# Attention with a sink: the sink as one more score column that TensorE writes, and queries scaled by ScalarE

## The reference, cut to what matters

```
sk = jnp.broadcast_to(sink...reshape(kv, g, 1, 1), s.shape[:-1] + (1,))
p = jax.nn.softmax(jnp.concatenate([s, sk], axis=-1), axis=-1)
return p[..., :-1]
```

## Time and profile before

| what | value |
|---|---|
| device time, median of 3 runs (lowest to highest) | 782.83 us (782.64 to 782.89) |
| device time of the profiled execution | 782.79 us |
| span, first to last instruction, in the profile | 780.9 us |
| mean granted TensorE clock | 0.996 |
| busy, PE / PEld / DVE / ACT / POOL | 738.8 / 573.5 / 583.1 / 502.8 / 50.4 us |

### The profile page before, as it was taken

The page is one execution under the profiler, slowest core; times in us unless marked ns, Lnnn a source line. Parts: engine busy times, 40 slices in busy tenths (PEclk is TensorE's granted clock), DMA queues, the critical chain, the costliest instruction groups (busy, mean ns, idle before and its releaser), DMA issues.

```text
span 780.9 us, 10972 instructions
## 1 busy us (share of the span) xinstructions
PE 738.8 (95%) x4019; PEld 573.5 (73%) x4020; DVE 583.1 (75%) x968; ACT 502.8 (64%) x834; POOL 50.4 (6%) x36
## 2 busy tenths in 40 slices
PE   4999999899999999999999999989999999999994
PEld 2557877457966888888769788845698788888874
DVE  4258386986666899999858746879666789999965
ACT  3048693574457777777646678457456887777852
POOL 0001352000000000000000135200000000000000
PEclk9999999999999999999999999999999999999998
DMA  9963034977338899999864113096831189999902
GB/s 365 423 244 109 14 121 168 423 271 272 109 116 366 316 369 366 379 368 350 327 240 153 58 52 103 33 382 211 303 128 55 55 327 379 375 363 376 370 18 84
DMA packets 33489, 186.26 MB, mean 239 GB/s; under 512 B 5136, under 2 KB 6288, under 8 KB 16400
## 3 DMA queue, kind: packets, MB, share of 16 engines
q1 hardware_dynamic: 33424, 185.42, 62.9%
HBM read 182.79 MB, written 2.62 MB: 237 GB/s over the span
## 4 chain that ended last, share of the span: by engine, by line
PE 74%; DVE 11%; ACT 9%; issue 4%; DMA 1%; ACTq 0%; DVEq 0%; SPq 0%
PE psum L875 22%; PE psum L1022 11%; PE psum L904 11%; PE psum L1224 5%; PE psum L989 4%; PE psum L705 3%; PE psum L927 3%; PE psum L853 2%; DVE att L2260 1%; ACT split L1415 1%; PE psum L741 1%; PE psum L1092 1%; PE psum L756 1%; PE psum L888 1%; PE psum L1106 1%
## 5 line engine op out<-in xcount | busy, mean ns | idle before, releaser
L2049 DVE TENSOR_TENSOR split<-ring,split 128x2048 fp32r<-128x2048 f32 x96 | 219.9, 2291 | 26.8 <-ACT split L1540 25.3
L1540 ACT CAST split<-ring 128x2048 fp32r<-128x2048 f32 x96 | 183.6, 1913 | 21.9 <-PE psum L904 14.5
L875 PE MATMUL psum<-split,y_hi 128*128 128x512 f32 x512 | 160.8, 395 | 0.4 <-ACT selT L1513 0.4
L875 PEld LDWEIGHTS psum<-split,y_hi 128*128 128x128 f32 x512 | 93.7, 188 | 18.6 <-issue 0.5
L875 PE MATMUL psum<-split,y_lo 128*128 128x512 f32 x256 | 100.1, 391 | 0.0
L1022 PE MATMUL psum<-ring_r,hT_hi 128*128 128x512 f32 x216 | 73.2, 393 | 0.0
L904 PE MATMUL psum<-split,hidT 128*128 128x512 f32 x256 | 69.7, 394 | 1.8 <-DVE hidT_lo L2054 1.8
L904 PEld LDWEIGHTS psum<-split,hidT 128*128 128x128 f32 x256 | 47.3, 188 | 14.2 <-DVE hidT_lo L2054 4.8
L875 PEld LDWEIGHTS psum<-split,y_lo 128*128 128x128 f32 x256 | 48.1, 188 | 10.2
L2490 POOL TENSOR_TENSOR ud<-const,da_hi 128x1024 fp32r<-128x1024 f32 x12 | 27.3, 2293 | 397.8 <-DVE da_lo L2150 390.3
L1022 PEld LDWEIGHTS psum<-ring_r,hT_hi 128*128 128x128 f32 x216 | 40.0, 188 | 9.0 <-issue 0.7
(11 more groups left out here) (314 smaller groups left out, 1425.6 us busy)
## 6 DMA issues: line engine op xcount, KB each, us to landing
ring<-in_w_gu SPq DMA_DIRECT2D x64, 1024.0 KB, 5.8
ring<-in_w_ada SPq DMA_DIRECT2D x40, 1024.0 KB, 6.6
ring<-in_w_down SPq DMA_DIRECT2D x32, 1024.0 KB, 5.7
ring<-in_w_rows SPq DMA_DIRECT2D x12, 1024.0 KB, 5.1
ring<-in_first SPq DMA_DIRECT2D x8, 1024.0 KB, 14.7
ring<-in_w_out SPq DMA_DIRECT2D x8, 1024.0 KB, 5.8
ring<-in_w_xbc SPq DMA_DIRECT2D x8, 800.0 KB, 9.1
par<-in_par SPq DMA_DIRECT2D x1, 1728.0 KB, 14.1
```

The source lines that it names most:

```text
L875: last = pe.matmul(dst, x[:, g, t, :], w[:, j, :], start=(t == 0 and i == 0), stop=(t == KD - 1 and i == 2))
L1540: act.copy(splits[unit_split(n)][:, 0, :], slot(key)).then_inc(raised("whi", l, p), 1)
L2049: tt(lo, slot(unit_key(l, p, n)), hi.bitcast(F32), ALU.subtract).then_inc(raised("wlo", l, p), 1)
```

## The change: the sink as a score column

A K = 1 matmul (ones by the sink) writes the sink into column w of the unit's bank, w being the number of keys, after the other matmuls of the pair have been issued. Maximum and exponential run over w + 1 columns where t = 0, so that the row sum holds the sink. The queries are scaled by 0.125 when ACT copies them, so that scores come out of TensorE with the factor in and the maximum is directly the bias of the exponential. The steps that handled the sink on DVE and ACT, the factor step, and the signal `es` are gone. Units with a sink need 385 columns for probabilities, so `probs` is a function: a tile that starts 16 words ahead of `hT`, in which slots 0 to 3 have 385 words each and slots 4 to 7 lie where they did.

```diff
+        with ExitStack() as shared:
+            prob_space = sb("prob_space", [P, 16 + KD * TOK], c=shared)
+        sb("prob_front", [P, 16])
...
-        nsink = sb("nsink", [P, DEPTH, NH])
...
-            att = sb("att", [P, 6, len(HEADS)], c=mix)
+            att = sb("att", [P, 3, len(HEADS)], c=mix)
...
-            probs = hT
+            def probs(u, a, b):
+                at = 12 + u % 8 * TOK + min(u % 8, 4)
+                return prob_space[:, at + a:at + b]
...
+            def sink(l, v, kv):
+                m, _, _, i = HEADS[2 * v]
+                w = P if m == 0 else TOK
+                at = T_SINK + 2 * kv + i
+                return pe.matmul(bank(("scores", l, 2 * v + kv))[:, w:w + 1], ones[0:1, :], tab[0:1, l, at:at + 1], start=False,
+                                 stop=True, skip_group_check=True)
...
@@ tensor, scores
-                            if m == 0:
+                            if m == 0 and t == 1:
                                 last.then_inc(*filled(("scores", l, 2 * v + kv)))
+                        if m == 0 and t == 0:
+                            for kv in range(NKV):
+                                sink(l, v, kv).then_inc(*filled(("scores", l, 2 * v + kv)))
...
                                 for kv in range(NKV):
-                                    last = pe.matmul(dsts[kv][:, other], ident_b, mask_b[:, m - 1, other], start=False,
-                                                     stop=True, skip_group_check=True)
-                                    last.then_inc(*filled(("scores", l, 2 * v + kv)))
+                                    pe.matmul(dsts[kv][:, other], ident_b, mask_b[:, m - 1, other], start=False,
+                                              stop=True, skip_group_check=True)
+                                for kv in range(NKV):
+                                    sink(l, v, kv).then_inc(*filled(("scores", l, 2 * v + kv)))
...
@@ scalar, turn_qk
-                            act.copy(qkT[:, 3 * t:3 * t + 3, m * P:(m + 1) * P], src).then_inc(*was_read(key))
+                            act.activation(qkT[:, 3 * t:3 * t + 2, m * P:(m + 1) * P], src[:, 0:2, :], ACT.Copy, scale=SCALE)
+                            act.copy(qkT[:, 3 * t + 2, m * P:(m + 1) * P], src[:, 2, :]).then_inc(*was_read(key))
@@ scalar, scores
-                        w = P if m == 0 else TOK
+                        w = (P if m == 0 else TOK) + (t == 0)
...
-                            act.activation(probs[:, u % 8, 0:w], src[:, 0:w], ACT.Exp, bias=att[:, 1, u:u + 1],
-                                           scale=SCALE, accum_out=att[:, 2, u:u + 1]).then_inc(*was_read(key))
-                        if t == 0:
-                            act.activation(att[:, 3, 2 * v:2 * v + 2], att[:, 3, 2 * v:2 * v + 2], ACT.Exp)\
-                                .then_inc(sig["es"], 1)
+                            act.activation(probs(u, 0, w), src[:, 0:w], ACT.Exp, bias=att[:, 0, u:u + 1],
+                                           accum_out=att[:, 1, u:u + 1]).then_inc(*was_read(key))
@@ vector, scores
-                            ins = dve.tensor_reduce(att[:, 0, u:u + 1], src[:, 0:P if m == 0 else TOK], AX.X, ALU.max,
-                                                    negate=True)
-                        ins.then_inc(dve_step, 1)
-                        dve.wait_ge(dve_step, dve_steps())
-                        if t == 0:
-                            sink = nsink[:, l, :].rearrange("p (v i) -> p i v", i=2)[:, i, :]
-                            stt(att[:, 1, two], att[:, 0, two], SCALE, sink, ALU.mult, ALU.min).then_inc(dve_step, 1)
-                            dve.wait_ge(dve_step, dve_steps())
-                            tt(att[:, 3, two], att[:, 1, two], sink, ALU.subtract).then_inc(sig["nb"], 1)
-                        else:
-                            ts(att[:, 1, two], att[:, 0, two], SCALE, None, ALU.mult).then_inc(sig["nb"], 1)
+                            ins = dve.tensor_reduce(att[:, 0, u:u + 1], src[:, 0:w], AX.X, ALU.max, negate=True)
+                        ins.then_inc(sig["nb"], 1)
@@ vector, scale
-                        den = att[:, 2, two]
-                        if t == 0:
-                            dve.wait_ge(sig["es"], per["es"] * l + sum(1 for x in range(v + 1) if HEADS[2 * x][1] == 0))
-                            tt(att[:, 4, two], den, att[:, 3, two], ALU.add).then_inc(dve_step, 1)
-                            dve.wait_ge(dve_step, dve_steps())
-                            den = att[:, 4, two]
-                        dve.reciprocal(att[:, 5, two], den).then_inc(dve_step, 1)
+                        dve.reciprocal(att[:, 2, two], att[:, 1, two]).then_inc(dve_step, 1)
...
-                            ins = ts(probs[:, u % 8, 0:w], probs[:, u % 8, 0:w], att[:, 5, u:u + 1], None, ALU.mult)
+                            ins = ts(probs(u, 0, w), probs(u, 0, w), att[:, 2, u:u + 1], None, ALU.mult)
```

More of the change, by code:

```diff
@@ L539, in build @@
                 ("dt_r", 1), ("da", 1), ("bss", 3), ("brs", 3), ("prep", 3), ("ud", 3), ("ud_lo", 3), ("da_lo", 1), ("xd", 3), ("yx", 3),
-                ("mhi", 4), ("mlo", 4), ("mixhi", 4), ("ohi", 1), ("olo", 1), ("wb", 3), ("dtd", 1), ("skip", 3), ("seg", 6), ("in_hi", PARTS + 2), ("in_lo", PARTS + 3), ("zs", 1), ("nb", PAIRS), ("es", PAIRS // 2), ("pn", PAIRS), ("yz", 1), ("yrs", 1), ("yn", 1),
+                ("mhi", 4), ("mlo", 4), ("mixhi", 4), ("ohi", 1), ("olo", 1), ("wb", 3), ("dtd", 1), ("skip", 3), ("seg", 6), ("in_hi", PARTS + 2), ("in_lo", PARTS + 3), ("zs", 1), ("nb", PAIRS), ("pn", PAIRS), ("yz", 1), ("yrs", 1), ("yn", 1),
                 ("flag", 1), ("top", 2), ("shares", 2), ("chosen", 2), ("hhi", 6),
@@ L1142, in _ @@
                             pe.wait_ge(setup_dve, 2)
+                            pe.wait_ge(par_in, 16)
                         if v in (0, 4):
@@ L1178, in _ @@
                             for c in range(1 if HEADS[u][0] == 0 else 3):
-                                last = pe.transpose(dst[:, c * P:(c + 1) * P], probs[:, u % 8, c * P:(c + 1) * P], ident)
+                                last = pe.transpose(dst[:, c * P:(c + 1) * P], probs(u, c * P, (c + 1) * P), ident)
                             last.then_inc(*filled(("turn", l, u)))
@@ L1930, in tables @@
                 dve.wait_ge(par_in, 16)
-                ts(nsink, tab[:, :, T_SINK:T_SINK + NH], -1.0, None, ALU.mult).then_inc(dve_step, 1)
-                dve.wait_ge(dve_step, dve_steps())
             def out_lo(l, n):
@@ L2254, in _ @@
                         v = arg[0]
-                        m, t, _, i = HEADS[2 * v]
-                        two = slice(2 * v, 2 * v + 2)
+                        m, t = HEADS[2 * v][0:2]
+                        w = (P if m == 0 else TOK) + (t == 0)
                         for u in (2 * v, 2 * v + 1):
@@ L2259, in _ @@
                             src = bank(("scores", l, u))
-                            ins = dve.tensor_reduce(att[:, 0, u:u + 1], src[:, 0:P if m == 0 else TOK], AX.X, ALU.max,
-                                                    negate=True)
-                        ins.then_inc(dve_step, 1)
-                        dve.wait_ge(dve_step, dve_steps())
-                        if t == 0:
-                            sink = nsink[:, l, :].rearrange("p (v i) -> p i v", i=2)[:, i, :]
-                            stt(att[:, 1, two], att[:, 0, two], SCALE, sink, ALU.mult, ALU.min).then_inc(dve_step, 1)
-                            dve.wait_ge(dve_step, dve_steps())
-                            tt(att[:, 3, two], att[:, 1, two], sink, ALU.subtract).then_inc(sig["nb"], 1)
-                        else:
-                            ts(att[:, 1, two], att[:, 0, two], SCALE, None, ALU.mult).then_inc(sig["nb"], 1)
+                            ins = dve.tensor_reduce(att[:, 0, u:u + 1], src[:, 0:w], AX.X, ALU.max, negate=True)
+                        ins.then_inc(sig["nb"], 1)
                     elif kind == "scale":
                         v = arg[0]
-                        m, t = HEADS[2 * v][0:2]
+                        m = HEADS[2 * v][0]
                         two = slice(2 * v, 2 * v + 2)
```

## The result

The change made the kernel slower: 790.08 us (median of seven executions, 786.62 to 791.59) against 782.83 (seven, 782.64 to 785.39). Ratio 1.0073, 95% interval 1.0059 to 1.0088. The forecast was 780.9, with a range of 779.0 to 783.4. The executions differ in their mean granted clock: the two at 0.996 took 786.6 and 786.7, the four at 0.990 and 0.991 took 790.1 to 791.6. The profiled execution took 790.08, with a span of 788.3.

The account below looks back on a forecast made before the run. DVE was taken as tight in the attention stage's first half, TensorE hardly looser; of 8.2 us taken from DVE three quarters go to TensorE's 5.3 of sinks, leaving 0.7 plus 1.2: 782.8 - 1.9 = 780.9 us, range 779.0 to 783.4.

Parts of the forecast that it names:

- DVE removed: Attention softmax: small sink and factor instructions go, 4.1 us of DVE's path per layer, 8.2 in all.
- widened: Maximum and exponential: one more column costs nothing (1.04 ns); ACT also loses its small exponential L1721 six times per layer.
- odd start: `probs` slots 1 and 3 start at an odd word; cost of scaling L2287 taken as 0, upper end 0.93 per layer.
- `turn_qk`: ACT's 384-column copy becomes 256 plus 128: +0.13 six times per layer, taken as 0; uncovered 0.8 per layer.
- rival 4: Scaling on DVE: odd start costs its double rate, 0.93 per layer, +1.0 in all, 781.9; chance 0.04.
- The sink pair: TensorE, attention: four passes at 0.11, 0.44 us a pair (ends 0.19 and 0.98), 5.3 us of new work.
- The stage: Attention followed wait by wait: gain 0.7 us in layer 0 and 1.2 in layer 1, sum 1.9.
- L2245 is not late here: Layer 1 attention: DVE's read of the SSD output isn't delayed by sinks, unlike layer 0, where the gain is lost.
- rival 1: Attention: TensorE takes it all back; a quarter of 7.2 us waiting stays, 1.8 of the gain goes, 782.7; chance 0.26.
- the three signs of being wrong: Sink pair over 0.6 us; L2287 on slots 1 and 3 near 0.6; TensorE's waits stay, busy time grows 5.
- I leave the clock out: Attention: granted clock is 1.00 in all four stretches and TensorE gets more work, so no clock effect was counted.
- Rival 3: TensorE, attention: sink passes don't overlap, 0.98 a pair, 0.54 more each; 785.2 to 787.4, about 786; chance 0.08.

Follow-up runs that it names:

- 5: As 2, with 26 never-executed DVE instructions in the jumped-over second expert pass, putting DVE's code where it lay before the change; 782.50 us, ratio 0.9997.
- 1: Kernel before, instructions unchanged, only its tiles moved to the SBUF places they have after the change; 789.62 us, ratio 1.0057.
- 2: Changed kernel with every tile of the matmuls again starting at a multiple of 128 bytes; 786.30 us, ratio 1.0028.
- 12: As 5, but all matmul tiles (front, mixer and experts) start 64 bytes past a multiple of 128; 782.25 us, ratio 0.9999.
- 9: Kernel before with 230 already-raised waits at the head of DVE's program, moving both jump and target; 804.42 us (two executions).
- 8: As 5, without sink matmuls: ACT takes the exponential of sink less maximum, DVE adds it to the row sum; 782.49 us, ratio 0.9983.
- 13: As 5, but all matmul tiles start 32 bytes past a multiple of 128; 788.70 us, ratio 1.0056.
- 7: As 5, with the sink written by one bf16 matmul per unit instead of an fp32 one with two passes; 778.89 us, ratio 0.9941.
- 10: As 5, but mixer and expert tiles 32 bytes past a multiple of 128, `hT`, ring and first two split buffers at 0; 786.87 us, ratio 1.0038.
- 14: As 5, but mixer and expert tiles 64 bytes past a multiple of 128, `hT`, ring and first two split buffers at 0; 788.59 us, ratio 1.0074.
- 3: Changed kernel with 96 bytes added: mixer and expert tiles at multiples of 128, `hT`, ring and splits still 64 past; 788.72 us, ratio 1.0073.
- 4: As 2, with the sink left out of the computation, maximum and exponential over the keys alone; 779.43 us, ratio 0.9931.
- 6: Kernel before with 230 waits in the jumped-over part, moving only the target of DVE's jump; 783.88 us, ratio 1.0004.
- 11: As 5, but `hT`, ring and first two split buffers 32 bytes past a multiple of 128, mixer and expert tiles at 0; 787.51 us, ratio 1.0064.
- 15: As 7 (bf16 sink, code position restored), with all tiles 64 bytes past a multiple of 128; 779.47 us, ratio 0.9946.

## Why the prediction was wrong, point by point

- **DVE removed, widened, odd start, `turn_qk`: right.** The instructions have gone; busy time 583.1 to 576.4; the scaling at odd starts 418 ns against 417, which settles rival 4 at nothing. The Trainium skill's rule in "Vector Engine (DVE) Microarchitecture Reference", section 5.1, is that 4-byte alignment makes no difference; an fp32 word at an odd place keeps that alignment, so the rule could not settle this case, as the prediction had it, and the 418 ns do. The two copies take 398 and 279 ns, 0.19 us more than the one of 488 where I had worked out 0.13; no wait of TensorE for them appeared.
- **The sink pair: mis-sized, 0.44, measured 0.53.** My 0.11 a pass came from six loads of one kind in a row; here it is 0.13, inside the ends 0.19 and 0.98. Twelve times 0.09 are 1.1 of the 1.9 us forecast.
- **The stage: 1.9 forecast, 0.8 measured** (5 against before: 0.19 and 0.65). TensorE's brackets in the stage add up to 4.22 and 5.39 us before, 0.82 and 2.10 in 5: 6.7 us of waiting lost, 6.4 filled with sinks. Single points in layer 0 of after came 0.6 to 0.9 behind the forecast, 0.2 of it because the stage began later: turn 2 at 146.89 (146.2 forecast), `ada_turn` at 150.02 (149.35), turn 5 at 154.89 (154.3), turn 8 at 165.38 (164.5). In layer 1, turn 2 still waits 1.28 in 5 where I had it 0.8 earlier. "L2245 is not late here" was wrong: DVE lost what it had gained by waiting for the second sink pair (L797) and for the SSD output (L1150) that TensorE issues behind the sinks:

```profile
513.80 0.52 DVE L2275 TENSOR_REDUCE att<-psum 128x1 f32<-128x129 f32 x2 [0.44 <-PE psum L797]
...
519.81 1.29 DVE L2260 TENSOR_TENSOR tmp<-psum,ex 128x512 f32<-128x512 f32 x2 [0.73 <-PE psum L1150]
...
523.79 0.44 PE L1199 MATMUL psum<-const,prob_space 128*128 128x128 f32 x2 [1.28 <-DVE prob_space L2287]
```

  For the stage alone rival 1, "TensorE takes it all back", was nearest in the number, but not by its reason: of the 7.2 us of waiting that had to go 6.7 went, so 0.5 stayed where that rival has 1.8; the dearer sinks took 1.1.
- **The step that failed: "After the stage the same chain of work follows in either kernel, so I expect the 1.9 to arrive at the end."** The chain was the same, its tiles and its code were not where they had been. The diff says that 64 bytes go in front of `hT` and 32 come out behind; I cost that at nothing without saying so, and experiments 1, 2 and 12 price it at 3.0. The 50 DVE instructions fewer (26 of them ahead of layer 1) moved the code to where DVE stands for 2.0 to 3.8 behind the jump between the layers; experiment 5 shows it, 9 supports it. None of the three signs of being wrong that the prediction names came true (the sink pair stayed under 0.6, the scaling at 418 ns, and TensorE's waits went); they all look inside the stage. Of the signs of being right two failed: "the rest of the span unchanged", and "both stages 0.5 to 1.5 us shorter" in layer 0 (0.2).
- **"I leave the clock out": wrong in most executions, cause open.** The fall costs 3.4 in the profiled execution. It happens without sinks (1), and the kernel before has clocks of 0.992 to 0.995 in 6 of 29 executions beside runs 5 to 8, so it was not brought by the change alone; after, it was 5 of 7 (0.990 to 0.995). In the profiled executions a fall in layer 1's attention cost 3.4 us in after, 1 and 13 and 1.7 in 2, 7, 10 and 14; there was none in the kernel before, 3, 4, 5, 6, 8, 9, 11, 12 and 15. So it came with places that cost time and with places that don't (2 and 7), and with and without sink matmuls; 1, 7 and 8 had another fall of 1.7, in or ahead of layer 0's expert stage. I found no single instruction or wait that brings it.
- **Rival 3, slower by exposed passes (0.98 a pair, 786):** its 786 is near the 786.6 measured at the higher clock, but by chance: what it rests on, 0.98 a pair, didn't happen.

The sum of the profiled execution: its span lies 9.3 us above what the forecast makes of it (780.9 less 1.9). That is 3.0 in the expert stages, 2.2 ahead of layer 1's attention, 3.5 in that attention (3.4 of them the clock), 0.5 in layer 0's attention and 0.1 in the other stretches.

## What to carry to other kernels

A change that adds or removes a small tile, or a few instructions on an engine, is also a change of every later address and of the code's position: list where the large operands start before and after, and look for "issue" gaps behind jumps, before costing such an edit at nothing. When work moves to an engine that is nearly full, compare its waits with the new work, term by term; 6.7 us of waits against 6.4 of sinks left nothing. A one-column fp32 matmul costs its two weight loads, and in bf16 it cost about a quarter of that.

## What the runs showed of the hardware that I had not expected

- The largest group of 128x512 matmuls (L875, L889, L890) took 395 or 396 ns on average with all tiles at 0 or all at 64 bytes past a multiple of 128, and 397 to 399 at the other places (where no fall of the clock lies in the stage), 1.2 to 1.8 us in a stage of 137; a mixture of 0 and 64 was among the others.
- DVE stood 1.46 to 3.80 us without a visible reason behind a jump, in every kernel with jump and target at 568 and 826 (counted in instructions from the start of DVE's program; after, 2, 3 and 4) and in the one with 824 and 1082; not at 568 and 852, 594 and 852, or 594 and 1082. ACT has an "issue" bracket of 2.38 to 2.88 us at the same jump in all seventeen kernels, 2.67 in the kernel before; no experiment touched it.
- Waits on semaphores that are long raised are not free: in 9 DVE spent 23.07 us on 230 such instructions, 0.100 each (the bracket of L1837).
- A one-column exponential took ACT 288 ns in 8, where a 128-wide one takes 363 in after and L1721, two columns wide, took 199 before; why stays open.
